# A two-layer decoder step: tiles written out, and the second layer's window attention taken block by block

## The reference, cut to what matters

```python
# second layer, for the prompt
z = rms_norm(x, norm_b[j]) @ w_in_b[j]
q, gq, qm, gm = jnp.split(z, [SWA_W, 2 * SWA_W, 2 * SWA_W + MEM_W], axis=-1)
q = rope_partial(rms_norm(q.reshape(B, T, N_Q_HEADS, HEAD_DIM), q_norm[j]), pos)
o = swa_banded(q, k, v, sinks[j])          # 12 heads, window 128, own and previous block of 128 keys
ys = o * jax.nn.silu(gq)
ym = memory_branch(qm, gm, mem_q_norm[li], mem_k[li], mem_v[li])   # 4 heads, 256 memory tokens
x = x + jnp.concatenate([ys, ym], axis=-1) @ w_out_b[j]
```

## Time and profile before

| | us |
|---|---|
| median of 3 runs | 1769.42 |
| the profiled execution | 1770.56 |
| its span | 1768.7 |
| PE busy | 1587.1 (90%) |
| DVE busy | 933.8 (53%) |
| ACT busy | 508.8 (29%) |
| POOL busy | 499.5 (28%) |
| mean granted clock of PE | 0.963 |

### The profile page before, as it was taken

The page is one execution under the profiler, slowest core; times in us unless marked ns, Lnnn a source line. Parts: engine busy times, 40 slices in busy tenths (PEclk is TensorE's granted clock), DMA queues, the critical chain, the costliest instruction groups (busy, mean ns, idle before and its releaser), DMA issues.

```text
span 1768.7 us, 33161 instructions
## 1 busy us (share of the span) xinstructions
PE 1587.1 (90%) x13448; PEld 1233.3 (70%) x13448; DVE 933.8 (53%) x1842; ACT 508.8 (29%) x1227; POOL 499.5 (28%) x353
## 2 busy tenths in 40 slices
PE   5778999899999999977989899999999999899976
PEld 2466887778788887854775757767576775767744
DVE  6876464445455454524663736556374563836531
ACT  2542223232323232211322414233142421514220
POOL 2631424142424132221313213132131412213120
PEclk9999999999999999988999999999999999999986
DMA  9021212212121213178001010100101001010041
GB/s 399 26 78 48 96 57 87 90 56 96 48 96 48 108 45 129 32 252 334 13 1 48 2 49 1 48 2 1 50 1 49 1 1 49 1 49 1 23 132 49
DMA packets 27417, 119.35 MB, mean 67 GB/s; under 512 B 3488, under 2 KB 3936, under 8 KB 16480
## 3 DMA queue, kind: packets, MB, share of 16 engines
q1 hardware_dynamic: 25184, 108.33, 16.4%
q10 hardware_dynamic: 2080, 8.80, 1.3%
HBM read 81.38 MB, written 37.64 MB: 67 GB/s over the span
## 4 chain that ended last, share of the span: by engine, by line
PE 38%; issue 36%; POOL 14%; DVE 7%; ACT 3%; DMA 2%; POOLq 0%; ACTq 0%; SPq 0%; DVEq 0%
PE ps_z L665 14%; PE ps_z L778 11%; POOL tiny_sb L2271 4%; PE ps_z L768 3%; POOL ph_sb L2427 2%; PE ps_z L836 2%; POOL pm_sb L2306 2%; POOL pm_sb L2295 2%; POOL big_sb L2276 1%; PE ps_z L654 1%; PE ps_p L748 1%; PE ps_t L738 1%; DVE w_in_sb L1621 1%; PE ps_p L954 1%; PE ps_p L1176 1%
## 5 line engine op out<-in xcount | busy, mean ns | idle before, releaser
L665 PE MATMUL ps_z<-xn_sb,w_in_sb 128*128 128x256 f16 (+1 forms) x4752 | 504.5, 265 | 4.9 <-DVE gate_sb L1676 3.8
L665 PEld LDWEIGHTS ps_z<-xn_sb,w_in_sb 128*128 128x128 f16 x4752 | 427.8, 98 | 62.7 <-issue 7.4
L778 PE MATMUL ps_z<-pm_sb,w_out_sb 128*128 128x256 f16 x2048 | 355.4, 276 | 19.2 <-DVE gate_sb L1702 15.9
L778 PE MATMUL ps_z<-gate_sb,w_out_sb 128*128 128x256 f16 x1024 | 283.0, 276 | 0.0
L2271 POOL TENSOR_TENSOR tiny_sb<-tiny_sb 128x2 f32<-128x2 f32 (+4 forms) x56 | 94.2, 1683 | 559.4 <-DVE tiny_sb L1643 317.4
L778 PEld LDWEIGHTS ps_z<-pm_sb,w_out_sb 128*128 128x128 f16 x2048 | 204.2, 100 | 48.8 <-issue 19.8
L654 PE MATMUL ps_z<-w_in_sb,xn_sb 128*128 128x512 f16 (+2 forms) x840 | 181.7, 376 | 0.0
L1634 DVE TENSOR_REDUCE tiny_sb<-scr_sb 128x8 f32<-128x512 f32 (+3 forms) x64 | 38.0, 594 | 247.7 <-ACT scr_sb L1202 163.3
L654 PEld LDWEIGHTS ps_z<-w_in_sb,xn_sb 128*128 128x128 f16 (+1 forms) x840 | 83.0, 99 | 94.1 <-issue 0.2
L1202 ACT ACTIVATE scr_sb<-ps_z,tiny_sb 128x256 f32<-128x256 f32 (+2 forms) x94 | 42.6, 489 | 361.2 <-PE ps_z L654 277.5
L1445 ACT ACTIVATE ph_sb<-ph_sb,tiny_sb 128x128 f32<-128x128 f32 x192 | 74.7, 390 | 134.2 <-DVE tiny_sb L2106 134.2
(11 more groups left out here) (267 smaller groups left out, 2377.4 us busy)
## 6 DMA issues: line engine op xcount, KB each, us to landing
x_buf_sb<-x SPq DMA_DIRECT2D x18, 1024.0 KB, 4.9
w_x_sb<-w_b SPq DMA_DIRECT2D x14, 1024.0 KB, 4.9
x<-x_buf_sb SPq DMA_DIRECT2D x9, 1024.0 KB, 3.9
y<-x_buf_sb SPq DMA_DIRECT2D x9, 1024.0 KB, 3.9
w_in_sb<-w_in_a SPq DMA_DIRECT2D x8, 1024.0 KB, 25.4
w_in_sb<-parts ACTq DMA_DIRECT2D x8, 1024.0 KB, 10.6
parts<-ph_sb SPq DMA_DIRECT2D x14, 512.0 KB, 3.0
parts<-w_x_sb SPq DMA_DIRECT2D x14, 512.0 KB, 3.1
```

Source lines behind the costliest of these rows:

```text
L665: last = mm(ps_z[:, b, half * NT:half * NT + n], w_split[:, g, ws, kc, half * P:(half + 1) * P], xs[:, x, kc, 0:n], start=(kc == 0 and ws ...
L778: last = mm(ps_z[:, b, half * NT:(half + 1) * NT], w_out_split[:, g, ws, kc, half * P:(half + 1) * P], gate_parts[x][:, kc, 0:NT], start=( ...
```

## The change

It has two parts.

1. All hardware loops become plain Python loops: every tile is written out on every engine. Waits compare with constants, and addresses are constants.
2. In the second layer the order of the steps is another one. `W6` takes block 0's three groups first and then block 1's. Groups 0 and 1 begin before PE has projected the last queries of block 1 (qb1), which is cut in two halves of 12 matmuls around `mem_scores` of block 0. The gate gm comes ahead of qb1. `q_heads` is cut into `first_queries` and `last_queries`. The output projection starts with the first third (0, 1) alone, in two halves, and takes (6, 7) after it.

```diff
-        W6 = [(0, 0), (1, 0), (0, 1), (1, 1), (0, 2), (1, 2)]
+        W6 = [(0, 0), (0, 1), (0, 2), (1, 0), (1, 1), (1, 2)]
...
-            "B": ["kv0", "kv1", "qa0", "qb0", "qa1", "qb1", "gm", "g0", "g1", "g2", *OUT],
+            "B": ["kv0", "kv1", "qa0", "qb0", "qa1", "gm", "qb1", "g0", "g1", "g2", *OUT],
...
-            "B": ["kT", "qT00", "qT01", "qT10", "qT11", "ptw0", "ptm00", "ptm01", "ptw1", "ptm10", "ptm11",
-                  "ptw2", "ptw3", "ptw4", "ptw5"],
+            "B": ["kT", "qT00", "qT01", "ptw0", "ptw1", "qT10", "qT11", "ptw2", "ptm00", "ptm01", "ptw3",
+                  "ptm10", "ptm11", "ptw4", "ptw5"],
...
-            "B": ["m0", "w0", "w1", "m1", "w2", "w3", "w4", "w5"],
+            "B": ["w0", "w1", "m0", "w2", "w3", "m1", "w4", "w5"],
...
-            with pe.Fori(0, TILES // 2) as it:
+            for it in range(TILES // 2):
...
+                    window_scores(t, p, 0)
+                    window_scores(t, p, 1)
+                    split_tokens("B", t, "qb1", P, w_split, (2, 3), kcs=range(0, 4))
                     T.wait_read(pe, "B", t, "qT01")
                     mem_scores("B", t, 0, qT_b, 6)
-                    window_scores(t, p, 0)
+                    split_tokens("B", t, "qb1", P, w_split, (2, 3), kcs=range(4, 8))
+                    window_scores(t, p, 2)
+                    window_transposes(t, 0)
+                    split_features("B", t, "g0", 4, halves=(0,))
+                    window_values(t, p, 0)
+                    window_transposes(t, 1)
+                    split_features("B", t, "g0", 4, halves=(1,))
                     q_transposes_b("B", t, 1, 0)
...
                     window_scores(t, p, 5)
-                    split_features("B", t, "g2", 6, halves=(1,))
-                    window_values(t, p, 3)
                     for g in range(4):
                         pe.wait_ge(wout_in[g], 32)
-                    window_transposes(t, 4)
-                    pe.wait_ge(glow_in.sem, glow_in.after("B", t, 1))
-                    split_out("B", t, 0, (0, 1, 6, 7), halves=(0,), first=True)
+                    pe.wait_ge(glow_in.sem, glow_in.after("B", t, 0))
+                    split_out("B", t, 0, (0, 1), halves=(0,), first=True)
                     window_values(t, p, 4)
                     window_transposes(t, 5)
-                    split_out("B", t, 0, (0, 1, 6, 7), halves=(1,), first=True)
+                    split_out("B", t, 0, (0, 1), halves=(1,), first=True)
+                    pe.wait_ge(glow_in.sem, glow_in.after("B", t, 1))
+                    split_out("B", t, 0, (6, 7))
...
+                    last_queries("B", t, 1, 6, angles("cos", 1), angles("sin", 1))
+                    window_weights(t, 0)
+                    window_front(t, 2)
                     mem_inverse("B", t, 0)
-                    window_back(t, 0)
+                    silu("B", t, "g0", 7, 0)
+                    window_gated(t, 0)
+                    window_weights(t, 1)
+                    window_back(t, 2)
...
+                    window_front(t, 5)
+                    gate_lows("B", t, 0, 0)
```

More of the change, by code:

```diff
@@ L552, in tile_a @@
                 dma(tile_of(x1d, t), x_buf[:, p]).then_inc(x_stored.sem, 16)
-            with sp.Fori(0, LOOPED // 2) as it:
+            for it in range(LOOPED // 2):
                 for q in range(2):
@@ L920, in _ @@
             tile_a(0)
-            with pe.Fori(0, LOOPED // 2) as it:
+            for it in range(LOOPED // 2):
                 for q in range(2):
@@ L1100, in _ @@
                     mem_transposes("B", t, 1, 0)
[L1101 removed]
+                    window_values(t, p, 3)
                     mem_transposes("B", t, 1, 1)
[L1103 to L1104 removed]
+                    window_transposes(t, 4)
                     mem_values("B", t)
[L1106 to L1108 removed]
@@ L1399, in _ @@
             tile_a(0, 0, x_arrived(1))
-            with act.Fori(0, LOOPED // 2) as it:
+            for it in range(LOOPED // 2):
                 for q in range(2):
@@ L1447, in window_exps @@
                 f(w_se[:, n % 2, :], w_sd[:, n % 2, :], ACT.Exp).then_inc(w_exp.sem, 1)
-            with act.Fori(0, TILES // 2) as it:
+            for it in range(TILES // 2):
                 for p in range(2):
@@ L1978, in _ @@
             own.loop(1 + 2 + 2 * 6)
-            with dve.Fori(0, LOOPED // 2) as it:
+            for it in range(LOOPED // 2):
                 for q in range(2):
@@ L2136, in _ @@
             own.loop(NBLK * (4 + 5) + 2 + 6 * 5 + 1)
-            with dve.Fori(0, TILES // 2) as it:
+            for it in range(TILES // 2):
                 for p in range(2):
@@ L2148, in _ @@
                     variance(k_ss, k_rstds[0]).then_inc(heads_var.sem, 1)
-                    for blk in range(NBLK):
-                        q_heads("B", t, blk, angles("cos", blk), angles("sin", blk))
+                    first_queries("B", t, 0, 2)
+                    last_queries("B", t, 0, 3, angles("cos", 0), angles("sin", 0))
+                    first_queries("B", t, 1, 4)
+                    silu("B", t, "gm", 5, 6)
+                    window_front(t, 0)
+                    window_front(t, 1)
@@ L2393, in _ @@
             own.loop(9)
-            with pool.Fori(0, LOOPED // 2) as it:
+            for it in range(LOOPED // 2):
                 for q in range(2):
@@ L2429, in _ @@
             own.loop(8)
-            with pool.Fori(0, TILES // 2) as it:
+            for it in range(TILES // 2):
                 for p in range(2):
```

138 lines of the change are left out of this document (62 added, 76 removed).

## The result

| | before | after |
|---|---|---|
| median, us (4 runs each, same chip) | 1769.90 (1767.92 to 1772.67) | 1853.96 (1846.36 to 1856.10) |
| ratio to before, 95% interval | | 1.047 (1.0453 to 1.0487) |
| the profiled execution, us | 1770.56 | 1856.1 |
| its span, us | 1768.7 | 1854.0 |
| PE busy | 1587.1 (90%) | 1613.9 (87%) |

The changed kernel is 84.1 us slower. The forecast was 1836, with a range to 1857: the sign and the range hold, and the number is 18 us too low.

A forecast was written before the change was run, and what follows sets the result against it. PE, busy 90% of the span, was taken as the bound. New waits +64, clock +17 and written-out loops -14.7 sum to +66 us, giving 1836 us; forecast 1825 to 1850, wider range 1813 to 1857.

The forecast's parts named there:

- loops written out: Both layers: holes where loops jump back, and the slow clock behind the first layer's, go; 14.7 us gained.
- new order, waits of PE: Second layer: new PE waits of 14.7 us per tile, less 6.7 already there; net 8.0 per tile, +64 us.
- clock: Second layer: PE's granted clock drops behind the two longest new waits, 1.4 us each; net 2.2 per tile, +17 us.
- rival 2: Written-out code gains nothing, since jumps are cheap or fetches come elsewhere; 1851 us, chance 0.06.
- Queries of block 0, values of group 0, memory weights 0 and 1: Four short PE waits per second-layer tile: 0.8 to 0.9, 0.8 to 1.2, 0.4 to 0.6 and 0.8 to 1.2 us.
- two bold waits: PE waits for DVE before block 1's first query transpose, 3.4 us, and before the first output projection, 3.9 to 4.1.
- Values of group 3: PE waits 1.4 to 1.8 us for a bank freed behind group 4's front, SiLU and gating.
- about 1.3 hidden in the modelled ends of the matmuls: Old waiting per tile, 0.16 us before each of eight waits, counted with 5.4 idle as 6.7 given back.
- a granted clock of 0.50 behind them: Sign of being right: clock at 0.50 behind the waits before L1012 (3.4 us) and L779 (4 us) in each second-layer tile.
- rival 3: Waits lengthen each other to 9 us per tile and the clock takes 33; +90 us, 1860, chance 0.14.
- Rival 1: The clock takes nothing more than today; +44 us, 1814, up to 1825 with part of it; chance 0.18.
- rival 4: It gets faster, as DVE is ahead at the two longest waits and they vanish; 1754 us, chance 0.04.

The follow-up runs named there:

- unroll_only: The kernel before with all ten loops written out and its order of steps kept; 1753.15 us, ratio 0.9912 to the kernel before.
- fill_three: The changed kernel with extra, overwritten matmuls in three waits per tile: before L1012, before L779 and before group 3's values; 1823.96 us, ratio 1.0314.
- unroll_fill: The kernel before, loops written out, old order, with 14 extra overwritten matmuls in its one 1.7 us wait per tile; 1751.65 us, ratio 0.9904.
- weights_early: The changed kernel with group 1's weights on DVE ahead of the SiLU of g0 and group 0's gating; 1837.53 us, ratio 1.0393.
- lows_early: The changed kernel with DVE's low half of the first third ahead of group 5's `window_front`; 1884.44 us, ratio 1.0662.
- three_early: The changed kernel with the first third's low half and the memory third's gating both ahead of group 5's `window_front` on DVE; 1881.67 us, ratio 1.0656.
- inverse_late: The changed kernel with `mem_inverse` of block 1 moved behind group 4's `window_front` on DVE; 1873.06 us, ratio 1.0597.
- fill: The changed kernel with 28 extra overwritten matmuls in the wait before L1012 and 34 in the wait before L779; 1839.71 us, ratio 1.0399.

## Why the prediction was right, and where it was off

The terms, each with what the runs give for it:

| term | predicted | measured | from |
|---|---|---|---|
| loops written out | -14.7 | -15.3 | unroll_only against before |
| new order, waits of PE | +64 (8.0 per tile) | +75 (9.4) | tiles of fill_three less tiles of unroll_fill, 918.6 - 843.5 |
| clock | +17 (2.2 per tile) | +26 (3.3) | tiles of after less fill_three, 29.2; less the 3.1 of unroll_only against unroll_fill |
| sum | +66 | +86 | 84.1 in the medians |

**Loops: right.** First layer: 7.5 us from tile 0 to tile 7 in unroll_only against 7.9. Second layer: 10.0 against 6.8. Two things came on top: the clock fell in fewer tiles (four behind tile 0 instead of six, 0.8 each), and every tile without a drop is 0.2 us shorter (105.21 against the 105.39 that the prediction took from tile 1), 1.4 over eight. The register work of the loops, which the prediction put at nothing, is the likely source of the second; no run takes it apart. A loop's end here costs PE about 2 us in the second layer and 6 to 7 in the first. The Trainium skill, "Advanced Engine Details and Errata", Control Flow Timing, has 51 and 108 ns for a branch; the trace disagrees with that as the price of a loop's end in this kernel. That rule was rival 2, and unroll_only is against it. What fills the hole no run here shows.

**Queries of block 0, values of group 0, memory weights 0 and 1:** 0.8, 1.2, 0.5 and 0.8 us; predicted 0.8 to 0.9, 0.8 to 1.2, 0.4 to 0.6, 0.8 to 1.2. Right.

**The two bold waits: right.** 3.4 before L1012 for L2128, and 4.1 before L779 for L1704. Their cause needs a finer word. For the first, weights_early shows that the SiLU and gating in front account for half only: had they not stood there, group 2's front would have held PE for 1.7, most of it through the one operation that took 1.40. For the second, the prediction named the low half behind `window_front` 5; lows_early and three_early show two further obstacles behind the same front, so in all three orders of DVE's queue that were tried 4 to 5 us stay, with group 5's chain as the last cause. What made it cost is what the prediction said last: PE has nothing else to do there. In the old order it had 4.1 us of g2, group 3's values and group 4's transposes.

**Values of group 3: the wait that was mis-sized.** Predicted 1.4 to 1.8, measured 2.4. The prediction has "whose bank is freed behind group 4's front (3.1)"; the front took 3.8, since its maximum took 1.31 instead of 0.69. In the old order no such POOL product stood beside this maximum; its line in the kernel before:

```profile
L2098 DVE TENSOR_TENSOR ph_sb<-ph_sb,lo_sb x48: 691/693/694, 863.1 to 1647.2; 128x512 f32<-128x512 f32 x48
```

The new order puts one beside group 4's front and one beside group 2's. I had taken each duration from the trace of before as if it were the instruction's own. That trace already showed otherwise: in tile 3 the operation of four columns at L2114, 0.15 to 0.16 us in 32 of its 48 places, takes 0.86 beside POOL's product and ends 0.02 us after it.

```profile
1185.95 0.86 DVE L2114 TENSOR_TENSOR tiny_sb<-tiny_sb 128x4 f32<-128x4 f32 x1 [1.13 <-ACT tiny_sb L1447]
```
```profile
1184.90 1.89 POOL L2306 TENSOR_TENSOR pm_sb<-pm_sb,tiny_sb 128x1024 f32<-128x1024 f32 x1 [3.89 <-DVE tiny_sb L1669]
```

The Trainium skill, "GPSIMD Engine Reference", Specifications, has GpSimd's SBUF interfaces shared with VectorE, with contention where a DVE instruction has two SBUF inputs. The trace agrees: all three slowed DVE operations have two, and inverse_late takes the overlap away and the maximum's 0.6 us with it.

**The sum of the waits: right, what was set against it: wrong.** Transposes of group 4 waited 0.8 (0.2 to 0.9). Those of group 5 show no wait in the changed kernel, since matmuls at half speed cover it; in the run fill, where they do not, it is 0.9 (0.8 to 0.9). All nine are then 0.8 + 1.2 + 3.4 + 2.4 + 4.1 + 0.5 + 0.8 + 0.8 + 0.9 = 14.9, or 14.7 with their second decimals, the sum that I took: what group 3's values had too much, the others stayed below their high ends. (The high ends of the prediction's list add to 15.0, not 15.2, and the upper end of its clock term to 32, not 33; the forecast hangs on neither.) But the tiles differ by 9.4 us and not 8.0, so only 5.3 is given back. The step that failed is "about 1.3 hidden in the modelled ends of the matmuls": the 5.4 us of idle time in rows 1 was all there was to give back. 8 x 1.3 = 10 us, over half of the miss.

**The clock: right in kind, 9 us short**, the rest of the miss. I priced two drops per tile at 1.4. Per tile the changed kernel has 6.8 or 13.7 us at half speed, by turns, in most tiles. Neither has the two drops of the forecast: tiles 2, 4 and 6 have one, of 6.8 us, at the wait before L779, and tiles 1, 3, 5 and 7 have three, since the third wait, of 2.4 us, draws one as well (in fill, where the other two are filled, in every tile). So "a granted clock of 0.50 behind them" holds at L779 in all tiles and at L1012 in five of eight. In the same way "114 to 117 us" holds in three tiles; four take 119.3 or 119.4, and tile 0 121.9. Each us at half speed cost 0.2 us (unroll_only, 0.8 for 3.4) to 0.46 (tiles 4 and 5 above, 3.14 for 6.9), less where part of it falls in a wait. The outcome is nearer to rival 3 (9 per tile and 33, 1860) than to my forecast's middle, and just outside the forecast's own 1825 to 1850. Of rival 3's two halves it is the clock that came, nearly; the waits did not lengthen each other beyond the 14.7 taken. Rival 1 is out, by the 29 us between after and fill_three; rival 4 too, by the waits.

## What to carry to other kernels

A wait that the old order covered need not go when the waited-for step moves up in its queue: here, before the first output projection, it went from the low half to a bank to a transpose, and kept its 4 to 5 us, because one chain (front, exponentials, product) stood behind it; look for what PE can do meanwhile, not for the queue. Durations read from one order hold only while the same engines run side by side. And changes whose effect is read at PE's clock should be measured with the clock held up by filler matmuls, once: waits and clock then come apart, in the profiled executions to 0.1 us per tile.

## What the runs showed of the hardware

- The same waits can cost different times: three_early's tiles 1 and 3, 115.99 and 122.88 us with equal waits, differ in time at half speed alone.
- The longest wait does not tell the cost: lows_early has none longer than 3.4 us, after has one of 4.1, their sums per tile are alike (14.5 and 14.7 us), and lows_early is 30 us slower, with 20.5 us at half speed in a tile against 6.8 or 13.7.
- How long a wait is does not say whether the clock falls: in unroll_only it fell at a wait of 1.7 us in four tiles and not in the other four; in the changed kernel it did not fall behind one of 3.4 us in three tiles of eight.
- A DVE operation of 128x4 took 1.40 us instead of 0.16 while POOL's product of 128x1024 ran, and ended with it. POOL's 2.90 us operation at L2278 did not do this: the maximum that ran beside its last 0.55 us in the changed kernel took 0.69.
- Extra matmuls in a wait make the kernel faster: 30 us with 82 of them in each tile.
